# Output weights split in place during the sparse attention, their second half read twice, and half of the first output tile's products issued from the first latent pass

## The chip, the core and the metric

The kernel runs on one core of a Trainium2 chip. A core has a matrix engine (TensorE, PE in the rows; PEld is its weight load), a vector engine (VectorE, DVE), a scalar engine (ScalarE, ACT), a general engine (GpSimd, POOL) and a queue for transfers (SyncE, SP), all with instruction streams of their own that meet only in semaphores. The metric is the device time of one launch in microseconds (us), as the median of several runs.

## What is computed

A decoder layer for 512 tokens of width 1024. One projection feeds two causal attentions of 8 heads each: A, where an indexer's scores pick 128 keys for each query, and B, the latent one, with queries and keys of 96 (64 + 32 rotary) channels. Both are gated, set side by side, multiplied by one output matrix and normalised:

```python
h = x @ w_in[l]
...
o_a = _dsa_branch(qa, ka, va, iq, ik, iw) * jax.nn.silu(ga)
o_b = _mla_branch(c_q, c_kv, k_rope, ...) * jax.nn.silu(gb)
out = jnp.concatenate([o_a, o_b], axis=-1) @ w_out[l]
x = _layernorm(DEEPNORM_ALPHA * x + out, ln_g[l], ln_b[l])
```

`w_out` is 1024 x 1024. Its rows 0 to 511 (chunks k = 0 to 3 of 128 rows) meet branch A's output, rows 512 to 1023 (k = 4 to 7) branch B's.

## The kernel before

Products of float32 accuracy are made of three products of a faster type: a matrix is split into a high part (a cast) and a low part (the value minus its high part), and high x high, high x low and low x high are added. So each weight chunk needs a cast and a subtraction before it can be used.

**Order of the work.** After the input projection (to about 170 us) the two attentions run as 64 units, one for each block of 128 queries and head: u = 0 to 31 for A (`NU_A` = 32), u = 32 to 63 for B. A pass is 8 units, one block m with all heads, and blocks come as m = 3, 2, 1, 0 (`ORDER`), each with m + 1 blocks of keys: 512, 384, 256, then 128 columns. Each engine has one loop over u, and its instruction order is fixed there. In iteration u, PE makes `scores(u)` (L1196 and L1199 in A, L1205 in B), `transposes(u - 2)` (L1255), `outputs(u - 4)` (L1271 in A, L1286 in B), and then output products if it is their turn. DVE masks the scores (`mask_unit`, L858; the scores come from PSUM, the mask from SBUF), in B also subtracts a low part (`probs_low`, L898), reads and merges head pairs (L913, L288), and once a pass normalises and gates (L874, L875, L884). ACT exponentiates (L583) and copies the transposes out (L603). `scores(u)` waits for `mask_unit(u - 2)`; transposes wait for the exponential.

**The output weights.** `w_out` comes in eight loads of 512 KB, one for each k, with two chunks j = 2k and 2k + 1 (its left and right 512 columns). They land in the ring `w_raw` (RING = 8 chunks of 2 KB a partition). The first four loads are issued at u = 8; the other four each wait until POOL has made the low parts of the ring slots that they overwrite. High parts `wo_hi`: of j = 0 to 7 by DVE in iterations 12 to 19 (`wo_high`, L936, one each), of j = 8 to 15 by ACT in iterations 38 to 45 (`split_hi`, L470). Low parts (`wo_lo_a`, `wo_lo_b`): all 16 by POOL (L431), which waits first until all 32 scores of A are made, since `wo_lo_a` and `wo_lo_b` lie where A's transposed keys lie.

**Output products.** For output tile i (one block of queries) PE makes 48 products (L1329), 8 chunks k x 2 halves x 3. Of tile 0 they stand in iterations 47 to 54 (`OUT_AT[0]` = 47), six in each, of tile 1 from 55, of tile 2 from 63. The operand `oT` is the gated output, transposed by `o_transposes` (L1300), then copied (ACT, L615) and its low part taken (DVE, L890); its first half (branch A) for tile 0 is made in iteration 45.

**POOL** has, in this order: rotary work of the latent queries, the low parts of B's values (`vb_parts`, L415, two operations), the 16 low parts of `w_out` with `scale_gate(0)` among them, then B's later pairs.

## Time and profile before

| | us |
|---|---|
| median of 3 runs | 321.32 (321.14 to 323.02) |
| profiled execution: span from first to last instruction | 318.7 |
| TensorE busy | 298.5 (94%) |
| VectorE busy | 248.5 (78%) |
| ScalarE busy | 177.9 (56%) |
| GpSimd busy | 146.0 (46%) |

The span is that of one profiled execution; the median holds in addition what lies around the first and last instruction. The chain that ended last goes through PE for 70% and through DVE for 18% of the span. Busy shares are means over stages with different limits, so the stretches of the two attentions are read apart.

### The profile page before, as it was taken

Reading aid. Unit: us, or ns where it says so; the run is one execution under the profiler, and the core shown is the slowest. Engines: PE = TensorE matmul, PEld = TensorE weight load, DVE = VectorE, ACT = ScalarE, POOL = GpSimd, SP = SyncE. Lnnn points to the kernel's source line nnn. Section 1 sums busy time; section 2 is a strip of 40 time slices with the busy share of each in tenths; the row PEclk is TensorE's granted clock in tenths of the full one; section 3 lists DMA queues with packets and bytes.
Section 4 is the critical chain, followed back from the end, with each engine's and each line's share of the span. In section 5 each row is a group of like instructions: output and inputs, shape, how many; then the busy total and the mean of one; then the engine's idle time right before and its main releaser. Section 6 shows DMA issues by size and latency. Waiting matters only on the chain.

```text
span 318.7 us, 5232 instructions
## 1 busy us (share of the span) xinstructions
PE 298.5 (94%) x1646; PEld 253.2 (79%) x1646; DVE 248.5 (78%) x613; ACT 177.9 (56%) x419; POOL 146.0 (46%) x163
## 2 busy tenths in 40 slices
PE   8869979999999999999999999999987899999991
PEld 7859968688888888887888789997654688888891
DVE  2968997888999999997053645865999967888685
ACT  5834244478234244366267787998878855554200
POOL 4858635310999994434326600020797310334311
PEclk9999999999999999999999999999999999999998
DMA  7947440300144433320055004230150340030311
GB/s 255 325 119 205 127 134 12 112 11 0 56 143 134 130 77 126 98 67 2 0 132 134 1 0 148 120 60 0 54 200 13 89 176 0 3 133 2 132 66 66
DMA packets 14202, 29.16 MB, mean 91 GB/s; under 512 B 1664, under 2 KB 4224, under 8 KB 14176
## 3 DMA queue, kind: packets, MB, share of 16 engines
q1 hardware_dynamic: 13904, 28.53, 29.0%
q10 hardware_dynamic: 272, 0.30, 0.3%
q8 instruction: 13, 0.21, 0.3%
q14 instruction: 13, 0.11, 0.1%
HBM read 24.18 MB, written 2.10 MB: 82 GB/s over the span
## 4 chain that ended last, share of the span: by engine, by line
PE 70%; DVE 18%; issue 4%; ACT 4%; DMA 2%; POOL 1%; DVEq 0%; SPq 0%; ACTq 0%; POOLq 0%
PE ps L1047 34%; PE ps L1329 14%; PE ps L1271 5%; PE ps L1255 5%; PE ps L1205 3%; PE ps L1196 2%; DVE tmp L731 2%; DMA w_raw<-in_w_in 2%; PE ps L1286 2%; PE ps L1199 2%; DVE tmp L732 1%; DVE idx_tok L734 1%; DVE trig_tmp L715 1%; DVE lat_tok L781 1%; DVE probsT_b L898 1%
## 5 line engine op out<-in xcount | busy, mean ns | idle before, releaser
L389 POOL TENSOR_TENSOR w_lo<-w_raw,w_hi 128x512 fp32r<-128x512 f32 (+3 forms) x62 | 76.1, 1245 | 47.3 <-ACT w_hi L470 47.3
L1047 PE MATMUL ps<-w_hi,x_hi 128*128 128x512 f32 (+2 forms) x220 | 83.2, 378 | 4.6 <-issue 3.7
L1047 PE MATMUL ps<-w_hi,x_lo 128*128 128x512 f32 (+2 forms) x220 | 82.0, 373 | 0.0
L1047 PE MATMUL ps<-w_lo,x_hi 128*128 128x512 f32 (+2 forms) x220 | 81.9, 372 | 0.0
L470 ACT ACTIVATE w_hi<-w_raw 128x512 fp32r<-128x512 f32 (+3 forms) x62 | 36.2, 592 | 68.9 <-PE ps L1047 68.0
L1047 PEld LDWEIGHTS ps<-w_hi,x_hi 128*128 128x128 f32 x220 | 41.4, 188 | 11.6 <-issue 5.0
L1047 PEld LDWEIGHTS ps<-w_hi,x_lo 128*128 128x128 f32 x220 | 41.3, 188 | 6.5
L1047 PEld LDWEIGHTS ps<-w_lo,x_hi 128*128 128x128 f32 x220 | 41.4, 188 | 5.9
L1329 PE MATMUL ps<-wo_hi,oT 128*128 128x512 f32 (+1 forms) x144 | 44.5, 371 | 0.0
L583 ACT ACTIVATE probs<-probs,small 128x512 f32<-128x512 f32 (+3 forms) x64 | 35.7, 559 | 11.7 <-DVE small L858 11.3
L1255 PE MATMUL ps<-ident,probs 128*128 128x128 f32 x160 | 28.5, 276 | 3.5 <-ACT probs L583 2.1
L1255 PEld LDWEIGHTS ps<-ident,probs 128*128 128x128 f32 x160 | 19.5, 140 | 14.6 <-DVE probsT_b L898 8.8
L1329 PEld LDWEIGHTS ps<-wo_hi,oT 128*128 128x128 f32 x144 | 26.1, 189 | 4.0
L812 DVE MATCH_REPLACE8 score<-small,score 128x256 f32<-128x256 f32 (+2 forms) x48 | 25.7, 550 | 0.0
L809 DVE MAX8 small<-score 128x8 f32<-128x256 f32 (+2 forms) x48 | 23.7, 555 | 0.0
L1205 PE MATMUL ps<-kbT,qbT 96*128 96x512 f32 (+3 forms) x64 | 23.2, 443 | 0.5 <-DVE small L858 0.5
L858 DVE CUSTOM_DVE_ANT_0 probs<-ps,causal 128x128 f32<-128x128 f32 (+3 forms) x40 | 17.7, 444 | 6.8 <-PE ps L1205 4.1
L858 DVE CUSTOM_DVE_ANT_0 probs<-ps,score 128x512 f32<-128x512 f32 (+2 forms) x24 | 13.3, 556 | 12.4 <-PE ps L1199 12.3
L415 POOL TENSOR_TENSOR vb_parts<-vb,vb_parts 128x512 fp32r<-128x512 f32 x2 | 2.9, 1470 | 42.3 <-ACT vb_parts L625 42.3
L1271 PE MATMUL ps<-va,probsT 128*128 128x64 f32 x160 | 21.4, 264 | 0.0
L1271 PEld LDWEIGHTS ps<-va,probsT 128*128 128x128 f32 x160 | 20.5, 193 | 0.6 <-issue 0.6
L288 POOL TENSOR_TENSOR obT<-half_sum,crossed 64x128 f32<-64x128 f32 x16 | 8.6, 538 | 26.8 <-DVE oT L890 15.6
(168 smaller groups left out, 583.3 us busy)
## 6 DMA issues: line engine op xcount, KB each, us to landing
w_raw<-in_w_in SPq DMA_DIRECT2D x20, 512.0 KB, 3.6
w_raw<-in_w_out SPq DMA_DIRECT2D x8, 512.0 KB, 4.3
kaT_swap<-kaT SPq DMA_DIRECT2D x8, 256.0 KB, 3.7
x_res<-in_x SPq DMA_DIRECT2D x4, 512.0 KB, 5.4
w_raw<-in_w_in SPq DMA_DIRECT2D x4, 416.0 KB, 4.1
x_raw<-in_xT SPq DMA_DIRECT2D x3, 512.0 KB, 5.5
out_y<-y SPq DMA_DIRECT2D x6, 256.0 KB, 2.0
w_raw<-in_w_in SPq DMA_DIRECT2D x3, 296.0 KB, 5.8
```

The costliest lines, as they stand in the source:

```text
L288: eng.tensor_tensor(obT[rows, g % 4], half_sum[rows, g % 2, a], crossed[rows, g % 2], ALU.add).then_inc(pair_merged, 1)
L389: pool.tensor_tensor(w_lo[:, s, 0:n], w_raw[:, s, 0:n], w_hi[:, s, 0:n], ALU.subtract).then_inc(w_lo_ready, 1)
L470: act.activation(dst, w_raw[:, s, 0:n], ACT.Copy).then_inc(w_hi_ready, 1)
L583: act.activation(probs[:, u % NPROBS, 0:N], probs[:, u % NPROBS, 0:N], ACT.Exp, bias=neg_max[:, u % 8:u % 8 + 1], scale=-1.0, accum_out=ro ...
L809: step(V.max(top8[:, 8 * j:8 * j + 8], sc))
L812: step(V.match_replace(out=sc, in_to_replace=top8[:, 8 * j:8 * j + 8], in_values=sc, imm_value=TAKEN))
L858: V.tensor_tensor_reduce(out=probs[:, u % NPROBS, 0:N], in0=ps_s[:, u % 2, 0:N], in1=bias, scale=-scale, scalar=3.0e38, op0=ALU.add, op1=A ...
L1047: ins = mm(dst, a, b, start=start and j == 0, stop=stop and j == len(pairs) - 1)
L1205: ins = mm(ps_s[:, b, 0:N], qbT[:, h, t], kbT[:, h, 0:N], start=True, stop=True)
L1255: ins = nc.tensor.transpose(bank[:, j * P:(j + 1) * P], probs[:, u % NPROBS, j * P:(j + 1) * P], ident[:, :])
L1271: ins = mm(ps_o[:, v % 2, h * A_DIM:(h + 1) * A_DIM], probsT[:, u % 3, j * P:(j + 1) * P], va[:, j, h * A_DIM:(h + 1) * A_DIM], start=(j = ...
L1329: ins = mm(out_ps(i, b), oT[i % 2][:, o, k, :], w[:, wcols], start=(r == 0), stop=(r == 3 * KT - 1))
```

## The change

- SP: after the first four loads of `w_out` come, at once, k = 4 and 5 into a new buffer `wo_early` (two chunk pairs), then the copy of the rotary keys (L334, L343 after), then k = 6 and 7 into the same buffer, each once DVE has cast the pair that lay there (`wo_hi_ready` of 10 and 12). When A's scores are made (u = 31 done), k = 4 to 7 are read a second time, into `wo_raw_b`, where A's keys lay, without further waits. 2 MB are read more.
- DVE casts all 16 chunks, in iterations 12 to 27 (before: 8 in 12 to 19). ACT casts none.
- POOL subtracts j = 0 to 7 in place in `w_raw` as soon as each is cast, ahead of the two `vb_parts` operations; j = 8 to 15 in place in `wo_raw_b`, behind them, then `scale_gate(0)`.
- The A half of tile 0: `o_transposes`, the ACT copy and the DVE low part stand in iteration 31 (`O_FIRST` + `T_LAG`; before 45), and its 24 products (k = 0 to 3, both halves) in iterations 34 to 41, three in each. Iterations 47 to 54 keep the other 24, three in each.
- `x_res`, `lng` and `lnb` move to other addresses; their loads follow the second reading.

```diff
-    O_AFTER = [NU_A + HEADS * (i + 1) + OT_AT - T_LAG for i in range(TT - 1)] + [NU]
+    O_AFTER = [[NU_A + HEADS * (i + 1) + OT_AT - T_LAG + b for b in range(2)] for i in range(TT - 1)] + [[NU, NU]]
+    O_AFTER[0][0] = O_FIRST
...
-    wo_lo_a = sb("wo_lo_a", 178, [P, KT // 2, 2, BANK], f32r)
+    wo_lo_a = sb("wo_lo_a", 64, [P, RING, BANK], f32r)
+    wo_early = sb("wo_early", 80, [P, 2, 2, BANK])
+    wo_raw_b = sb("wo_raw_b", 98, [P, KT // 2, 2, BANK])
...
+        def out_steps(i):
+
+            split = ((0, KT // 2), (KT // 2, KT)) if i == 0 else ((0, KT),)
+            return [(b, k, j) for k0, k1 in split for b in range(len(PIECES[i])) for k in range(k0, k1) for j in range(3)]
...
+            sp.wait_ge(acc_ready, A_END)
+            for k in range(KT // 2, KT):
+                if k >= KT // 2 + 2:
+                    sp.wait_ge(wo_hi_ready, 2 * k - 2)
+                sp.dma_start(wo_early[:, k % 2], w_out_v[:, k]).then_inc(early_loaded[k % 2], 16)
+                if k == KT // 2 + 1:
+                    sp.wait_ge(acc_read[2], ACC_LAST[2])
+                    sp.dma_start(kbT[NOPE:B_QK, 1:B_HEADS, :],
...
-            for q in range(C_OUT // 2 + RPAIR, len(LOADS)):
-                load(q)
-            sp.wait_ge(w_lo_ready, C_OUT + 2 * KT)
+            sp.wait_ge(scores_ready, NU_A)
+            for k in range(KT // 2, KT):
+                sp.dma_start(wo_raw_b[:, k - KT // 2], w_out_v[:, k]).then_inc(raw_b_loaded[k - KT // 2], 16)
...
+            for j in range(KT):
                 c = C_OUT + j
                 pool.wait_ge(w_loaded[(c // 2) % RPAIR], 16 * (c // 2 // RPAIR + 1))
-                wait_wo_hi(pool, j)
-                if j == 0:
-                    pool.wait_ge(scores_ready, NU_A)
+                pool.wait_ge(wo_hi_ready, j + 1)
                 pool.tensor_tensor(wo_lo(j // 2, j % 2), w_raw[:, c % RING, :], wo_hi[:, j // 2, j % 2],
                                    ALU.subtract).then_inc(w_lo_ready, 1)
-                if j == SCALE_AT:
-                    scale_gate(0)
...
+            for j in range(KT, 2 * KT):
+                k = j // 2
+                pool.wait_ge(raw_b_loaded[k - KT // 2], 16)
+                pool.wait_ge(wo_hi_ready, j + 1)
+                pool.tensor_tensor(wo_lo(k, j % 2), wo_raw_b[:, k - KT // 2, j % 2], wo_hi[:, k, j % 2],
+                                   ALU.subtract).then_inc(w_lo_ready, 1)
+            scale_gate(0)
...
-                if 0 <= u - WO_LATE < RING:
-                    split_hi(C_OUT + RING + u - WO_LATE)
...
-                V.tensor_copy(wo_hi[:, j // 2, j % 2], w_raw[:, c % RING, :]).then_inc(wo_hi_ready, 1)
+                if k < KT // 2:
+                    dve.wait_ge(w_loaded[(c // 2) % RPAIR], 16 * (c // 2 // RPAIR + 1))
+                    src = w_raw[:, c % RING, :]
+                else:
+                    dve.wait_ge(early_loaded[k % 2], 16 * ((k - KT // 2) // 2 + 1))
+                    src = wo_early[:, k % 2, j % 2]
+                V.tensor_copy(wo_hi[:, k, j % 2], src).then_inc(wo_hi_ready, 1)
...
-                if 0 <= u - WO_EARLY < RING:
+                if 0 <= u - WO_EARLY < 2 * KT:
                     wo_high(u - WO_EARLY)
...
+                if 0 <= u - A_HALF_AT < HEADS:
+                    out_products(0, 3 * (u - A_HALF_AT), 3 * (u - A_HALF_AT + 1))
                 for t in range(TT - 1):
                     if 0 <= u - OUT_AT[t] < HEADS:
-                        out_products(t, per * (u - OUT_AT[t]), per * (u - OUT_AT[t] + 1))
+                        rest, first = (per, 0) if t > 0 else (per // 2, 3 * KT)
+                        out_products(t, first + rest * (u - OUT_AT[t]), first + rest * (u - OUT_AT[t] + 1))
...
+O_FIRST = 29
+A_HALF_AT = 34
```

VectorE in iterations 20 to 22 of the sparse attention, before (the two ISA rows are one mask with its read-out):

```order
L858 ISA probs,small<-ps,score 128x256
L858 ISA small 128x1
L874 RECIPROCAL small<-small 128x8
L875 TENSOR_TENSOR o_norm<-ps,small 128x512
L858 ISA probs,small<-ps,score 128x256
L858 ISA small 128x1
L884 TENSOR_TENSOR gate<-o_norm,gate 128x512
L858 ISA probs,small<-ps,score 128x256
L858 ISA small 128x1
```

and the same place of the changed kernel:

```order
L868 ISA probs,small<-ps,score 128x256
L868 ISA small 128x1
L884 RECIPROCAL small<-small 128x8
L885 TENSOR_TENSOR o_norm<-ps,small 128x512
L951 CAST wo_hi<-wo_early 128x512
L868 ISA probs,small<-ps,score 128x256
L868 ISA small 128x1
L894 TENSOR_TENSOR gate<-o_norm,gate 128x512
L951 CAST wo_hi<-wo_early 128x512
L868 ISA probs,small<-ps,score 128x256
L868 ISA small 128x1
L951 CAST wo_hi<-wo_early 128x512
```

Each of the iterations 20 to 27 has gained a cast behind its mask. GpSimd from the last rotary operation to the first pair, before:

```order
L415 TENSOR_TENSOR vb_parts_94<-vb,vb_parts_94 128x4x128
L415 TENSOR_TENSOR vb_parts_93<-vb,vb_parts_93 128x4x128
L431 TENSOR_TENSOR wo_lo_a<-w_raw,wo_hi 128x512 x8
L431 TENSOR_TENSOR wo_lo_b<-w_raw,wo_hi 128x512 x5
L423 TENSOR_TENSOR gate<-gate,small 128x512
L431 TENSOR_TENSOR wo_lo_b<-w_raw,wo_hi 128x512 x3
```

and now:

```order
L434 TENSOR_TENSOR wo_lo_a<-w_raw,wo_hi 128x512 x8
L438 TENSOR_TENSOR vb_parts_96<-vb,vb_parts_96 128x4x128
L438 TENSOR_TENSOR vb_parts_95<-vb,vb_parts_95 128x4x128
L444 TENSOR_TENSOR wo_lo_b<-wo_raw_b,wo_hi 128x512 x8
L428 TENSOR_TENSOR gate<-gate,small 128x512 x2
```

Eight subtractions have moved ahead of the value parts, from the latent attention into the sparse one. PE in iteration 35, now with three output products behind the outputs (before, the score row followed directly):

```order
L1222 MATMUL ps<-kbT,qbT 128x512
L1272 MATMUL ps<-ident,probs 128x128 x4
L1288 MATMUL ps<-va,probsT 128x64
L1345 MATMUL ps<-wo_hi,oT_66 128x512
L1345 MATMUL ps<-wo_lo_a,oT_66 128x512
L1345 MATMUL ps<-wo_hi,oT_66 128x512
```

The same three rows stand in each of the iterations 34 to 41, and 24 rows are gone from iterations 47 to 54.

## Rows read from the trace of the kernel before

**Rows 1.** Head of the page.

```profile
span 318.7 us, 5232 instructions
```

**Rows 2.** Busy time by stretch; (x) counts instructions, then PE's granted clock and transfers.

```profile
core 0: us, PE busy (x) PEld busy (x) DVE busy (x) ACT busy (x) POOL busy (x), PEclk, DMA share, GB/s
202.00:219.60 17.60, 17.42 (x152) 16.90 (x151) 13.03 (x54) 15.94 (x56) 1.67 (x1) 1.00 0.14 27
...
222.00:237.40 15.40, 14.14 (x80) 9.32 (x78) 14.29 (x31) 12.58 (x32) 12.52 (x10) 1.00 0.30 103
237.40:249.35 11.95, 9.37 (x50) 6.07 (x51) 11.42 (x28) 11.08 (x30) 9.09 (x8) 1.00 0.13 46
...
253.10:270.70 17.60, 17.60 (x100) 15.09 (x99) 12.75 (x38) 9.89 (x30) 1.05 (x1) 1.00 0.31 108
```

**Rows 3.** VectorE in order of time, iterations 12 to 28: start, duration, line, operation, count, [idle before].

```profile
202.04 0.43 DVE L936 CAST wo_hi<-w_raw 128x512 fp32r<-128x512 f32 x1
...
202.98 0.69 DVE L884 TENSOR_TENSOR gate<-o_norm,gate 128x512 f32<-128x512 f32 x1
...
210.44 0.42 DVE L858 CUSTOM_DVE_ANT_0 probs<-ps,score 128x256 f32<-128x256 f32 x1 [0.36 <-PE ps L1199]
...
212.57 0.42 DVE L858 CUSTOM_DVE_ANT_0 probs<-ps,score 128x256 f32<-128x256 f32 x1
...
214.02 0.29 DVE L858 CUSTOM_DVE_ANT_0 probs<-ps,causal 128x128 f32<-128x128 f32 x1 [0.44 <-PE ps L1199]
...
217.25 0.29 DVE L858 CUSTOM_DVE_ANT_0 probs<-ps,causal 128x128 f32<-128x128 f32 x1 [0.46 <-PE ps L1199]
```

**Rows 4.** VectorE and GpSimd side by side, in order of time.

```profile
33.77 1.41 POOL L389 TENSOR_TENSOR w_lo<-w_raw,w_hi 128x512 fp32r<-128x512 f32 x1 [0.92 <-ACT w_hi L470]
34.05 1.27 DVE L755 CAST iq_st<-idx_tok 128x256 fp32r<-128x256 f32 x1
...
226.12 10.46 POOL L431 TENSOR_TENSOR wo_lo_a<-w_raw,wo_hi 128x512 fp32r<-128x512 f32 x8
230.03 0.68 DVE L898 TENSOR_TENSOR probsT_b<-ps,probsT_b 128x512 fp32r<-128x512 f32 x1
230.63 1.03 DVE L884 TENSOR_TENSOR gate<-o_norm,gate 128x512 f32<-128x512 f32 x1
```

**Rows 5.** Operations on `wo_hi`: ns min/median/max, first and last start.

```profile
L936 DVE CAST wo_hi<-w_raw x8: 419/421/427, 202.0 to 209.7; 128x512 fp32r<-128x512 f32 x8
L431 POOL TENSOR_TENSOR wo_lo_a<-w_raw,wo_hi x8: 1267/1279/1732, 226.1 to 235.3; 128x512 fp32r<-128x512 f32 x8
L470 ACT ACTIVATE wo_hi<-w_raw x8: 612/614/616, 233.0 to 249.3; 128x512 fp32r<-128x512 f32 x8
```

**Rows 6.** Pair merges, VectorE: ns min/median/max of one; two of them from the timeline.

```profile
L288 DVE TENSOR_TENSOR obT<-half_sum,crossed x16: 282/290/1264, 234.8 to 268.3; 64x128 f32<-64x128 f32 x16
...
239.77 1.03 DVE L288 TENSOR_TENSOR obT<-half_sum,crossed 64x128 f32<-64x128 f32 x2
...
243.74 1.55 DVE L288 TENSOR_TENSOR obT<-half_sum,crossed 64x128 f32<-64x128 f32 x2
```

**Rows 7.** Two pieces of the chain that ended last: start, length, what.

```profile
246.62 0.50 ACT wo_hi L470
...
251.85 1.38 PE ps L1329 x6
```

**Rows 8.** PE: scores of iterations 42, 47 and 48, from the timeline.

```profile
237.38 0.91 PE L1205 MATMUL ps<-kbT,qbT 96*128 96x384 f32 x2 [0.50 <-DVE small L858]
...
249.35 0.81 PE L1205 MATMUL ps<-kbT,qbT 96*128 96x384 f32 x2
...
253.07 0.59 PE L1205 MATMUL ps<-kbT,qbT 96*128 96x256 f32 x2
```

**Rows 9.** Transfers: KB each, median us from issue to landing.

```profile
w_raw<-in_w_in SPq DMA_DIRECT2D x20, 512.0 KB, 3.6
...
lnb<-in_ln_b SPq DMA_DIRECT2D x1, 512.0 KB, 6.4
```

More of the change, by code:

```diff
@@ L165, in wo_lo @@
     def wo_lo(k, half):
-        return (wo_lo_a if k < KT // 2 else wo_lo_b)[:, k % (KT // 2), half]
+        return wo_lo_a[:, (C_OUT + 2 * k + half) % RING] if k < KT // 2 else wo_lo_b[:, k - KT // 2, half]
     def y_of(i):
@@ L197, in build @@
         pos_loaded, norm_g_loaded, ln_loaded = sem("pos_loaded"), sem("norm_g_loaded"), sem("ln_loaded")
+        early_loaded = [sem(f"early_loaded{i}") for i in range(2)]
+        raw_b_loaded = [sem(f"raw_b_loaded{i}") for i in range(KT // 2)]
         xres_loaded = [sem(f"xres_loaded{i}") for i in range(2)]
@@ L423, in scale_gate @@
                 pool.tensor_tensor(g3, g3, rinv.unsqueeze(2).broadcast_to([P, HEADS, V_DIM]), ALU.mult).then_inc(gate_scaled, 1)
[L425 removed]
+            for j in range(KT):
                 c = C_OUT + j
                 pool.wait_ge(w_loaded[(c // 2) % RPAIR], 16 * (c // 2 // RPAIR + 1))
[L428 to L430 removed]
+                pool.wait_ge(wo_hi_ready, j + 1)
                 pool.tensor_tensor(wo_lo(j // 2, j % 2), w_raw[:, c % RING, :], wo_hi[:, j // 2, j % 2],
                                    ALU.subtract).then_inc(w_lo_ready, 1)
[L433 to L434 removed]
+            for j in (3, 2):
+                pool.wait_ge(vb_hi_ready, VB_ORDER.index(j) + 1)
+                pool.tensor_tensor(vb_parts[j][:, :, 1:3], vb[:, j, :].rearrange("p (q a d) -> p q a d", a=2, d=V_DIM),
+                                   vb_parts[j][:, :, 0:4:3], ALU.subtract).then_inc(vb_lo_pool, 1)
+            for j in range(KT, 2 * KT):
[5 more added lines that the diff above has]
+            scale_gate(0)
             def root(i):
@@ L462, in split_hi @@
                 act.wait_ge(w_loaded[(c // 2) % RPAIR], 16 * (c // 2 // RPAIR + 1))
-                if c >= C_OUT:
-                    k, half = divmod(c - C_OUT, 2)
-                    dst = wo_hi[:, k, half]
-                else:
-                    dst = w_hi[:, s, 0:n]
-                    if c >= RING:
-                        wait_chunk_used(act, c - RING)
+                dst = w_hi[:, s, 0:n]
+                if c >= RING:
+                    wait_chunk_used(act, c - RING)
                 act.activation(dst, w_raw[:, s, 0:n], ACT.Copy).then_inc(w_hi_ready, 1)
@@ L606, in copy_oT_hi @@
                 n = slot_of[i, b]
+                if i == 0 and b == 0:
+                    act.wait_ge(wo_hi_ready, 2 * KT)
                 if i >= 2 and b == 0:
@@ L639, in _ @@
                 i, j = divmod(u - NU_A, HEADS)
-                if 0 < i < TT and j == OT_AT:
+                if u == O_FIRST + T_LAG:
+                    copy_oT_hi(0, 0)
+                if 1 < i < TT and j == OT_AT:
                     copy_oT_hi(i - 1, 0)
@@ L997, in _ @@
                     evac_qpeT(u - PET_AT - 1)
-                if 0 <= u - WO_EARLY < RING:
+                if 0 <= u - WO_EARLY < 2 * KT:
                     wo_high(u - WO_EARLY)
-                if 0 < i and j == OT_AT:
+                if u == O_FIRST + T_LAG:
+                    copy_oT_lo(0, 0)
+                if 1 < i and j == OT_AT:
                     copy_oT_lo(i - 1, 0)
@@ L1303, in out_products @@
             def out_products(i, a, z):
-                last = i == TT - 1
+                last, steps = i == TT - 1, out_steps(i)
                 for n in range(a, z):
-                    b, r = divmod(n, 3 * KT)
-                    k, j = divmod(r, 3)
+                    b, k, j = steps[n]
+                    r = 3 * k + j
                     cols = PIECES[i][b]
@@ L1314, in out_products @@
                         pe.wait_ge(oT_lo_ready, 2 * i + 1 + (k > 0))
-                    if n == 0:
-                        if i == 0:
-                            pe.wait_ge(w_lo_ready, C_OUT + 2 * KT)
+                    if i == 0 and n in (0, 3 * KT):
+                        pe.wait_ge(w_lo_ready, C_OUT + (KT if n == 0 else 2 * KT))
                     if r == 0:
```

32 lines of the change are left out of this document (10 added, 22 removed).

## The prediction

> **What bounds the kernel now.** I read the page first (span 318.7 us [rows 1]), then busy time by stretch, then the timelines of the two attentions, and last the chain of waits at the seams.
>
> In the sparse attention, iterations 12 to 31, TensorE is busy 17.42 of 17.60 us [rows 2] and sets the pace. VectorE has small gaps there: in iterations 20, 24 and 28 it waited 0.36, 0.44 and 0.46 us for scores ahead of its mask [rows 3]. That is the cover for anything added to VectorE. GpSimd is nearly empty, 1.67 us.
>
> The latent attention has three parts. Iterations 34 to 41 are the stretch from 222.0 to 237.4, where the scores of 42 begin [rows 8]: TensorE is busy 14.14 of 15.40 us, idle 1.26 [rows 2]. Iterations 42 to 46 take 11.95 us for five, 2.39 each, with TensorE busy only 9.37 and VectorE 11.42, ScalarE 11.08 [rows 2]: this is the hole. The chain there runs through ScalarE's cast of `wo_hi`, 0.50 us a time [rows 7], and through VectorE's work. Iteration 47 takes 3.72 us (249.35 to 253.07 [rows 8]). Iterations 48 to 54, seven of 17.60 us in sum, 2.51 each, are TensorE's again: 17.60 busy of 17.60 [rows 2], 1.38 us of each being six output products [rows 7].
>
> **What the change takes from the sparse attention.** Three terms.
>
> (a) GpSimd now subtracts while VectorE casts. The two don't overlap: a cast of 128x256 that began at 34.05 under a GpSimd subtraction (33.77 to 35.18) took 1.27 us and ended 0.14 after it; the gate of 230.63 took 1.03 instead of 0.69 beside GpSimd, while the low part at 230.03, which reads PSUM, took its usual 0.68 [rows 3, 4]. One of the merges of 290 ns took 1264 [rows 6]. The mask reads PSUM too, so it is not held up; the casts and the gate are. The Trainium skill, SBUF — State Buffer, section Who interferes with whom, says that a cast in a two-port mode or a VectorE operation with two SBUF inputs shares a port pair with GpSimd, and the first to start has it for its whole instruction. By that rule all the 128x512 casts are held up, which is a wider claim than the one 128x256 cast that the trace shows; were they not, the sum would be that of the first rival below.
>
> Each subtraction waits for its cast and then runs 1.279 us [rows 5]; the next cast comes behind one mask, 0.5 us later, and finds GpSimd at work. So cast and subtraction alternate: 1.28 plus 0.27 (twice the 0.14, for twice the width) to 0.42 (a whole cast [rows 5]), 1.55 to 1.70; I take 1.62. The first subtraction starts at 202.5 (cast 0 at 202.04 [rows 3]) and ends at 203.8; the gate, due at 202.98, ends at 204.4 behind it, cast 1 at 204.7, and cast 7 six rounds later at 204.7 + 6 x 1.62 = 214.4. The mask of iteration 20 follows cast 7. It stood at 210.44 [rows 3]: +4.0 us. With 1.55 and 1.70 it is +3.5 and +4.5; TensorE can't hide it, since scores of u wait for the mask of u - 2, and it has no other work.
>
> (b) In iterations 20 and 21, cast 8 waits for subtraction 7 (ends about 215.7), so it ends at 216.0. The value part, now behind the eight, takes GpSimd then for 1.3 us and the gate of iteration 21 waits for it (217.4, ending at 218.0), then cast 9, 218.3. The mask of 22 follows: 218.3 - 214.4 = 3.9 us after that of 20, where it was 212.57 - 210.44 = 2.1 [rows 3]. +1.8 us; bounds 0.5 (two casts bare, 0.84, less one gap) and 2.6.
>
> (c) k = 6 may be loaded only after cast 9, and cast 12 needs it. A 512 KB load takes 3.6 us to land, up to 6.4 [rows 9]. Issued at 218.4 it lands at 222.0. Iteration 24's mask would stand at about 219.7 (1.45 us after that of 22, as 214.02 - 212.57 [rows 3]) and its cast at 220.0: it waits 2.0 us, and behind it on VectorE wait the masks of 25 and 26, for which TensorE's scores wait. k = 7, issued after cast 11 (219.7), lands at 223.3, about when cast 14 comes. From there four casts and masks at VectorE's pace bring mask 28 to about 224.4, 4.7 us after mask 24, where it was 217.25 - 214.02 = 3.2 [rows 3]: +1.5; bounds 0.8 and 4.3 (6.4 us to land).
>
> (d) The moved transposes, copy and low part of iteration 31 cost up to 0.7 on VectorE; TensorE's lead over the masks at the end gives about as much back. In sum 4.0 + 1.8 + 1.5 = 7.3, less 0.3 for TensorE's lead: **+7.0**, bounds 4.5 and 11.
>
> The other additions are free. The loads of k = 4 and 5 are needed ten iterations later. The second reading goes out when A's scores are made, at 219.6 in the old count [rows 2], where GpSimd is through with the value parts at 226.1 [rows 4]; 6.5 us are more than one load takes. The eight late subtractions lie under iterations 34 to 41, where VectorE will have slack. Without that cover they would cost what they do now, some 1.4 us.
>
> **What it gives back in the latent attention.** The 24 moved products are 0.23 us each (1.38 for six [rows 7]), 0.69 an iteration.
>
> - Iterations 34 to 41: +5.5 us of products, into 1.3 us of idle time [rows 2]; modelled ends hide some more idle time. **+3.7**, bounds 3.2 and 4.3. This half of the work moves from a full TensorE to a full TensorE.
> - Iterations 42 to 46: ScalarE loses five casts of 0.61 [rows 5] and is no bound. VectorE's 11.42 us hold about 1.4 us of waiting on GpSimd (two pairs of merges, 1.03 and 1.55 us instead of 0.6 [rows 6]) and 0.7 for the low part moved away: 9.35, 1.87 an iteration, against TensorE's 1.4 (2.51 less 1.38 is 1.13 for 256 keys; for 384 I estimate 0.3 more). So VectorE sets 9.35 against 11.95: **-2.6**, bounds -1.6 and -3.6.
> - Iteration 47: 3.72 becomes about 2.0 (TensorE's 1.3, between 1.13 and 1.4, and 0.69). **-1.7**.
> - Iterations 48 to 54: 2.51 - 0.69 = 1.82. VectorE has 12.75 us in seven, 1.82 as well [rows 2], so not all of 7 x 0.69 = 4.8 comes: **-4.2**, bounds -2.5 and -4.8.
>
> Sum: +3.7 - 2.6 - 1.7 - 4.2 = **-4.8**, bounds -1.5 and -6.9. Tiles 1 to 3 and the tail are unchanged.
>
> **The sum.** 318.7 + 7.0 - 4.8 = 320.9 us of span. The median of the runs shown, 321.32, is 2.6 us over the span of the profiled execution, so 323.5.
>
> **The rivals.**
>
> 1. *The casts slip by GpSimd.* Then (a) and (b) fall to the gaps: eight more casts of 0.34 to 0.42 in iterations with 0.4 us of slack, about +0.5; cast 12 comes at 214.4, its load, issued at 211.4, lands at 215.0, +1.0 for both late loads; 0.3 for iteration 31. +1.8 - 4.8 = -3.0 with the low bound of the gain, -5.1 with the high one: 316 to 318. For it: none of the 128x512 casts has been seen under GpSimd. Against: [rows 4]. Chance 0.20, with the case that the gain is at its upper bound.
> 2. *VectorE stays the bound of the latent attention*, the other side. The place is iterations 42 to 54: where VectorE needs 2.0 us in 42 to 46 and 2.2 in 48 to 54, since it also waits for ScalarE's copies in each round, the gain there is 2.0 + 1.5 + 2.1 = 5.6 against +3.7, -1.9 in sum: 318.7 + 7.0 - 1.9 + 2.6 = 326.4. It decides from 0.15 us an iteration more than I take. For it: VectorE busy 11.42 of 11.95. Chance 0.20.
> 3. *The loads of k = 6 and 7 are late.* At 6.4 us each, (c) is 4.3 instead of 1.5: 326.3. Against: nothing else moves then. Chance 0.10.
> 4. *The change does not do what it says*: the products move between two full stretches and the hole stays, because it was VectorE's and not ScalarE's. Then 42 to 46 stay at 11.9: 326.1. Chance 0.05.
>
> **How the numbers follow.** My forecast, 322 to 324.5 and down to 318 where (b) and (c) are at their low bounds, has 0.45. About 1% (3.2 us) is what a measurement of this kernel can tell from no change. Faster by over 1% (under 318.1) is rival 1, 0.20. Slower (over 324.5) are rivals 2, 3 and 4, 0.35. The range goes from 317.5 (most of rival 1 left in) to 328 (two of the slower bounds together left out).
>
> **What would show it.** (a) right: the casts of iterations 13 to 19 last 1.0 to 1.3 us in the rows instead of 0.42, GpSimd's subtractions alternate with them, and the mask of iteration 20 starts near 214.4. (b): the gate of iteration 21 at over 1 us. (c): VectorE idle 1 to 2 us on a transfer ahead of cast 12. The latent attention: iterations 34 to 41 near 19 us, 42 to 46 near 9.4, 48 to 54 near 13.4, no ScalarE cast in the chain. TensorE's idle time should have moved from 237-249 to 204-224. I am wrong if the casts stay at 0.42 under GpSimd, or if the first score of B starts before 224 or after 230 (it was 219.6).

## The result, and the profile after

The changed kernel takes **329.46 us** (median, 328.48 to 334.31) against 321.63 (321.14 to 323.02) before: a ratio of 1.0222, interval 1.0175 to 1.0269. It is slower, by 7.8 us, clear of noise; the forecast was 323.5 with a range up to 328. One of its four executions, 334.31, ran in a slower state at a lower mean clock (0.961, against 0.974 to 0.981 in the others), and the median of the other three is 329.19. The profiled execution has a span 8.7 us longer than that of [rows 1]. In every execution the time is 1.8 or 1.9 us over the span, so differences of medians and of spans can be compared.

The page's head, and its rows of TensorE's busy share and granted clock in 40 equal slices of 8.2 us (9 is 90% or more):

```profile
span 327.4 us, 5237 instructions
PE   7869989999999999999999999878999979899990
...
PEclk9979999999999999999999999998799999999998
```

TensorE's idle time does move, out of the latent attention into the slices at 205 to 229 us, as forecast. What the forecast had nothing of is the second row: behind those slices the granted clock drops.

Busy time by stretch, columns as in [rows 2]; the first row answers to the first of [rows 2]:

```profile
202.00:219.60 17.60, 15.07 (x111) 12.85 (x109) 17.47 (x34) 11.64 (x34) 11.46 (x9) 1.00 0.31 96
...
219.70:226.37 6.67, 4.72 (x36) 4.22 (x37) 3.71 (x19) 3.87 (x16) 0.00 (x0) 0.97 0.48 157
226.37:233.78 7.41, 7.41 (x29) 5.65 (x30) 3.89 (x16) 4.83 (x19) 0.00 (x0) 0.57 0.47 168
233.78:252.69 18.91, 18.91 (x103) 14.05 (x103) 15.25 (x35) 13.03 (x32) 11.67 (x9) 1.00 0.44 157
252.69:260.26 7.57, 7.55 (x47) 5.76 (x46) 7.21 (x23) 6.72 (x20) 1.05 (x1) 1.00 0.02 3
260.26:264.90 4.64, 2.49 (x14) 1.57 (x13) 4.34 (x11) 3.38 (x9) 0.00 (x0) 1.00 0.00 0
264.90:277.61 12.71, 12.71 (x78) 11.05 (x77) 9.93 (x30) 8.66 (x26) 1.05 (x1) 1.00 0.00 0
```

VectorE is now the full engine of the sparse attention (17.47 of 17.60 us, before 13.03) and TensorE has gaps (15.07, before 17.42). The second row is masks 22 to 28, the third mask 28 to score 34, and the last four are iterations 34 to 41, 42 to 46, 47, and 48 to 54. By iteration, with the forecast beside it (up to iteration 28 between starts of masks on VectorE, from 34 on between starts of scores on TensorE; all in us):

| stage | before | after | difference | forecast |
|---|---|---|---|---|
| up to mask 2 | 183.35 | 184.42 | +1.07 | 0 |
| masks 2 to 13 | 19.15 | 19.15 | 0 | 0 |
| masks 13 to 20 (a) | 7.94 | 12.40 | +4.46 | +4.0 |
| masks 20 to 22 (b) | 2.13 | 3.73 | +1.60 | +1.8 |
| masks 22 to 28 (c) | 4.68 | 6.67 | +1.99 | +1.5 |
| mask 28 to score 34 (d) | 4.77 | 7.41 | +2.64 | -0.3 |
| scores 34 to 42 | 15.36 | 18.91 | +3.55 | +3.7 |
| scores 42 to 47 | 11.97 | 7.57 | -4.40 | -2.6 |
| scores 47 to 48 | 3.72 | 4.64 | +0.92 | -1.7 |
| scores 48 to 55 | 17.49 | 12.71 | -4.78 | -4.2 |
| scores 55 to 56 | 2.29 | 3.41 | +1.12 | 0 |
| the rest | 45.85 | 46.38 | +0.53 | 0 |

The differences make 8.7 us, the forecast column 2.2. So 6.5 us are to be explained, and most of them lie in five rows: (d) 2.9, iteration 47 2.6, iteration 55 1.1, the start 1.1, and in the other direction iterations 42 to 46 with 1.8.

**The sparse attention.** VectorE in order of time, columns as in [rows 3]:

```profile
204.05 1.46 DVE L894 TENSOR_TENSOR gate<-o_norm,gate 128x512 f32<-128x512 f32 x1
...
206.24 1.30 DVE L951 CAST wo_hi<-w_raw 128x512 fp32r<-128x512 f32 x1
207.47 0.54 DVE L868 CUSTOM_DVE_ANT_0 probs<-ps,score 128x384 f32<-128x384 f32 x1
...
207.94 1.31 DVE L951 CAST wo_hi<-w_raw 128x512 fp32r<-128x512 f32 x1
...
223.11 0.43 DVE L951 CAST wo_hi<-wo_early 128x512 fp32r<-128x512 f32 x1 [1.76 <-DMA wo_early<-in_w_out]
...
225.49 0.43 DVE L951 CAST wo_hi<-wo_early 128x512 fp32r<-128x512 f32 x1 [1.19 <-DMA wo_early<-in_w_out]
```

and GpSimd beside it:

```profile
205.99 1.27 POOL L434 TENSOR_TENSOR wo_lo_a<-w_raw,wo_hi 128x512 fp32r<-128x512 f32 x1 [1.03 <-DVE wo_hi L951]
207.69 1.27 POOL L434 TENSOR_TENSOR wo_lo_a<-w_raw,wo_hi 128x512 fp32r<-128x512 f32 x1 [0.43 <-DVE wo_hi L951]
209.39 1.27 POOL L434 TENSOR_TENSOR wo_lo_a<-w_raw,wo_hi 128x512 fp32r<-128x512 f32 x1 [0.43 <-DVE wo_hi L951]
```

Six of the eight casts of j = 0 to 7, 0.42 us each before [rows 5], take 1.30 to 1.44 under GpSimd; the other two (0.43 and 0.41) met no subtraction. The gate of 0.69 takes 1.46, while the mask between them, which reads PSUM, keeps its 0.54. Cast and subtraction alternate in a cycle of exactly 1.70 us (207.69, 209.39): 1.27 of subtraction and 0.43 until the next one. The cast of 206.24 ends at 207.54, 0.28 behind the end of the subtraction that it met, and the next subtraction begins 0.15 later. The two transfers of 1.76 and 1.19 us are the late k = 6 and 7.

**The clock.** PE's granted clock around the seam, busy time by stretch again:

```profile
220.00:224.00 4.00, 3.06 (x25) 2.81 (x25) 2.23 (x12) 2.61 (x10) 0.00 (x0) 1.00 0.71 223
224.00:226.00 2.00, 1.47 (x12) 1.22 (x11) 0.81 (x5) 1.04 (x6) 0.00 (x0) 0.98 0.20 78
226.00:232.00 6.00, 5.83 (x22) 4.60 (x23) 3.48 (x15) 3.84 (x15) 0.00 (x0) 0.50 0.32 108
232.00:234.00 2.00, 2.00 (x10) 1.47 (x9) 1.00 (x3) 1.42 (x4) 0.00 (x0) 0.81 0.87 332
```

For 6.8 us (225.9 to 232.8) TensorE ran at the lower of its two levels, 1.2 instead of 2.4 GHz, in iterations in which it sets the pace again. It had been idle for 4.3 of the 23 us before, in gaps of 0.2 to 0.5 us and around the two late loads. In the kernel before, the clock is 1.00 throughout these stretches.

**Iteration 47.** TensorE in order of time:

```profile
261.65 0.60 PE L1303 MATMUL ps<-probsT_b,vb_parts 128*128 128x256 f32 x3
264.13 0.47 PE L1345 MATMUL ps<-wo_hi,oT 128*128 128x512 f32 x1 [1.88 <-issue]
```

and the chain of waits there (start, length, what):

```profile
261.93 0.03 ACT probsT_b L611
261.95 0.36 issue
262.31 0.63 ACT oT L625
262.94 1.18 issue
264.13 0.93 PE ps L1345 x3
```

The first product of iteration 47 is now k = 4, the first that needs the B half of `oT`. That half is copied in the same iteration (262.31 on ScalarE) and its low part taken behind it (263.35 to 264.03 on VectorE). Before the change the twelve products of k = 0 to 3 came first, in iterations 47 and 48: there, in the trace of before, the low part of the B half was ready at 253.63 and its first product (k = 4) began at 256.70:

```profile
252.95 0.68 DVE L890 TENSOR_TENSOR oT<-obT,oT 128x512 fp32r<-128x512 f32 x1
...
256.70 0.40 PE L1329 MATMUL ps<-wo_hi,oT 128*128 128x512 f32 x1
256.93 0.40 PE L1329 MATMUL ps<-wo_lo_b,oT 128*128 128x512 f32 x1
```

Now the six products have become three, and the gap in front of them is 1.88 us.

### The profile page after: what moved, and what is told of

The parts are those of the page before. It is cut to its first block, busy times and chain, and to the rows that moved or that the text cites. A ratio compares the mean times of both kernels' runs of the same rounds, so it can differ in the third digit from the quotient of the medians.

```text
span 327.4 us, 5237 instructions
## 1 busy us (share of the span) xinstructions
PE 304.0 (93%) x1646; PEld 257.8 (79%) x1646; DVE 254.6 (78%) x621; ACT 175.4 (54%) x411; POOL 145.4 (44%) x163
## 4 chain that ended last, share of the span: by engine, by line
PE 69%; DVE 18%; issue 5%; DMA 3%; SPq 1%; ACT 1%; POOL 1%; DVEq 0%; ACTq 0%; POOLq 0%
PE ps L1064 36%; PE ps L1345 13%; PE ps L1222 5%; PE ps L1272 4%; PE ps L1288 3%; PE ps L1303 3%; DVE wo_hi L951 2%; DMA w_raw<-in_w_in 2%; DVE probs L868 2%; DVE tmp L741 2%; DVE tmp L742 1%; DMA wo_early<-in_w_out 1%; PE ps L1213 1%; DVE lat_tok L791 1%; DVE iq_st L765 1%
## 5 line engine op out<-in xcount | busy, mean ns | idle before, releaser
L1064 PE MATMUL ps<-w_hi,x_lo 128*128 128x512 f32 (+2 forms) x220 | 82.9, 377 | 0.0
L1064 PEld LDWEIGHTS ps<-w_hi,x_hi 128*128 128x128 f32 x220 | 42.1, 191 | 11.8 <-issue 6.0
L1345 PE MATMUL ps<-wo_hi,oT 128*128 128x512 f32 (+1 forms) x144 | 46.1, 373 | 1.9 <-issue 1.9
L1064 PEld LDWEIGHTS ps<-w_hi,x_lo 128*128 128x128 f32 x220 | 42.0, 191 | 6.5
L819 DVE MAX8 small<-score 128x8 f32<-128x256 f32 (+2 forms) x48 | 23.5, 545 | 0.0
L1288 PEld LDWEIGHTS ps<-va,probsT 128*128 128x128 f32 x160 | 21.5, 200 | 0.9 <-issue 0.9
L1288 PE MATMUL ps<-va,probsT 128*128 128x64 f32 x160 | 22.2, 271 | 0.0
L434 POOL TENSOR_TENSOR wo_lo_a<-w_raw,wo_hi 128x512 fp32r<-128x512 f32 x8 | 10.2, 1274 | 25.3 <-DVE wo_hi L951 25.3
L611 ACT ACTIVATE probsT_b<-ps 128x512 fp32r<-128x512 f32 (+3 forms) x32 | 13.8, 431 | 12.5 <-PE ps L1272 12.2
```

What stands on the lines that cost most here:

```text
L611: act.activation(dst, ps_pT[:, slot_of[u] % 2, 0:N], ACT.Copy).then_inc(probsT_copied, 1)
L819: step(V.max(top8[:, 8 * j:8 * j + 8], sc))
L1064: ins = mm(dst, a, b, start=start and j == 0, stop=stop and j == len(pairs) - 1)
L1288: ins = mm(ps_o[:, v % 2, h * A_DIM:(h + 1) * A_DIM], probsT[:, u % 3, j * P:(j + 1) * P], va[:, j, h * A_DIM:(h + 1) * A_DIM], start=(j = ...
L1345: ins = mm(out_ps(i, b), oT[i % 2][:, o, k, :], w[:, wcols], start=(r == 0), stop=(r == 3 * KT - 1))
```

## The experiments

My theory after the two traces: four losses, each with a place of its own. Casts and subtractions exclude each other (a), the loads of k = 6 and 7 are late (c), TensorE's gaps then bring its clock down (d), and iteration 47 waits for copies that its old products used to hide. Against it stand single causes: the clock falls because of the late loads or of the transfers at the seam; and the latent attention gains nothing from the products, only from ScalarE's lost casts. The stages below are those of the table. Each stage time comes from the one profiled execution of its kernel; the name in brackets is the one by which the expectations call a kernel.

**All sixteen subtractions late.** (`e1_late_sub`)

```diff
+            vb_low_pool(3)
+            pool.wait_ge(scores_ready, NU_A)
             for j in range(KT):
...
-            for j in (3, 2):
...
+                if j == 3:
+                    vb_low_pool(2)
...
-A_HALF_AT = 34
+A_HALF_AT = 40
```

> The changed kernel with GpSimd's eight early subtractions held back until all scores of the sparse attention are made (the value parts before and between them), and the first half's products in iterations 40 to 47 instead of 34 to 41, so that they have their low parts. Port theory (casts and gate on VectorE and subtractions on GpSimd exclude each other; cost 4.5 us in iterations 12 to 20 and 1.6 in 20 to 22): the casts fall to 0.42 us, the mask of iteration 20 comes about 7.9 us after that of 13 instead of 12.4, and the median falls by 6 us to about 323.5; to 321 if TensorE's clock then stays up as well. The late loads still cost about 2 us. GpSimd is then busy beside the merges of the latent attention, up to 1.5 us back. Rival (the second reading or the moved products make the loss): within 1 us of 329.5.

324.25 us (323.65 to 325.12), ratio 1.0081 (1.0055 to 1.0107). Casts in the sparse attention, ns min/median/max:

```profile
L955 DVE CAST wo_hi<-w_raw x8: 420/422/427, 204.3 to 211.9; 128x512 fp32r<-128x512 f32 x8
L955 DVE CAST wo_hi<-wo_early x8: 414/420/426, 213.9 to 222.7; 128x512 fp32r<-128x512 f32 x8
```

Masks 13 to 20 take 7.94 us, as before the change: (a) is the exclusion and nothing else, since the casts in these iterations are the same as before. The clock stays at 1.00 from 204 to 232 and mask 28 to score 34 takes 5.10. The two late loads remain (1.73 and 1.09 us), so a load wait alone did not bring the clock down here. This is the profiled execution, with a mean clock of 0.986; four of the other five had 0.970 to 0.980, so the clock was lower for longer in those, and where in them is not known. (b) remains too, 3.77 us, without any subtraction:

```profile
214.39 1.28 POOL L432 TENSOR_TENSOR vb_parts<-vb,vb_parts 128x512 fp32r<-128x512 f32 x1 [31.19 <-DVE wo_hi L955]
...
214.56 1.64 DVE L898 TENSOR_TENSOR gate<-o_norm,gate 128x512 f32<-128x512 f32 x1
```

GpSimd's first value part began 0.17 us ahead of the gate, which took 1.64 instead of 0.69. In return iterations 42 to 46 take 11.86 us instead of 7.57: their products stand there now, and GpSimd subtracts beside the merges.

**Value parts two iterations later** (`e7_late_sub_vb22`), on top of it.

```diff
-VB_EARLY = 20
+VB_EARLY = 22
```

> As e1_late_sub (all sixteen subtractions late), but GpSimd's two value parts are let go two iterations later (VB_EARLY 22 for 20). In e1_late_sub the mask of iteration 22 stood 3.77 us behind that of 20 (2.13 before); there GpSimd's first value part (1.28 us) had begun 0.17 us ahead of the gate, which took 1.64. My theory: that collision is most of the 1.6 us: iterations 20 to 22 fall to 2.1 to 2.6, and the median from 324.25 to about 322.8. Rival (the casts of iterations 20 and 21 themselves, which stand behind gate and read-out, make the time): 20 to 22 stays at 3.5 or more and the median at 324.2.

324.01 us (322.82 to 324.80), ratio 1.0073 (1.0052 to 1.0095). The gate took 0.69 and masks 20 to 22 fell from 3.77 to 2.81 (I had 2.1 to 2.6), so 0.96 of (b)'s 1.6 us is that one collision; the 0.7 that is left goes with the two casts behind read-out and gate. The median moved by 0.2 only: in the profiled execution the granted clock now dipped (0.73 in 220 to 224, 0.68 in 224 to 226 us) and mask 28 to score 34 took 6.18 instead of 5.10. My place was right, my forecast of the time missed.

**Four subtractions early, twelve late** (`e8_four_early`), against the kernel with all of them late.

```diff
-            vb_low_pool(3)
-            pool.wait_ge(scores_ready, NU_A)
             for j in range(KT):
...
                 if j == 3:
+                    vb_low_pool(3)
+                    pool.wait_ge(scores_ready, NU_A)
                     vb_low_pool(2)
```

> As e1_late_sub, but the first four subtractions stand beside the casts as in the changed kernel, the other twelve late. It tells the price of one round and where the granted clock begins to fall. My theory (price in proportion): iterations 13 to 20 take 7.94 plus the gate's 0.9 plus three to four rounds of 0.4 to 0.5, about 10.2 (12.40 with eight, 7.94 with none); the granted clock stays at 1.00 since TensorE's idle time is half that of the changed kernel; median about 326. Rival (any idle time there brings the clock down): the granted clock shows 0.5 somewhere between 218 and 235 us and the median is 327.5 or more.

325.94 us (323.98 to 327.40), ratio 1.0121 (1.0079 to 1.0164). Masks 13 to 20: 9.85, between 7.94 and 12.40. The gate took 1.45, three casts 1.30, 1.31 and 1.44, the next 0.42: the price is by the collision. The median is what I expected, but the clock was my miss: in the profiled execution it stood at 0.50 from 225.3 to 235.6 us. The four executions ran from 323.98 at a mean clock of 0.991 to 327.40 at 0.972, so the fall seems to come in some executions of this kernel and not in others.

**Loads of k = 4 and 5 first** (`e2_reload_early`), casts in the order 8 to 11, 0 to 7, 12 to 15, so that k = 6 and 7 are loaded long before their casts.

```diff
+CAST_ORDER = [8, 9, 10, 11, 0, 1, 2, 3, 4, 5, 6, 7, 12, 13, 14, 15]
...
-                    wo_high(u - WO_EARLY)
+                    wo_high(CAST_ORDER[u - WO_EARLY])
```

> The changed kernel with the casts in the order j = 8 to 11, 0 to 7, 12 to 15 and the loads of k = 4 and 5 issued first, so that those of k = 6 and 7 go out eight iterations sooner. Late-load theory: VectorE's two waits for wo_early (1.76 and 1.19 us) vanish, -2.0. Clock theory (the granted clock fell to 0.50 from 225.9 to 232.5 us because TensorE had stood still between 216 and 226): the clock stays at 1.00 there and another 2.3 us go, 325.2. Rival (that fall of the clock is chance, or comes from the exclusion alone): 327.5. The port cost of 6 us stays in either case.

326.98 us (326.28 to 328.01), ratio 1.0166 (1.0128 to 1.0204). The waits for transfers are gone, and masks 13 to 28 take 20.45 instead of 22.80. The clock fell all the same, earlier:

```profile
216.00:220.00 4.00, 2.48 (x17) 1.98 (x16) 4.00 (x8) 1.74 (x6) 2.55 (x3) 0.97 0.00 0
220.00:224.00 4.00, 4.00 (x21) 4.00 (x21) 4.00 (x13) 2.20 (x9) 3.05 (x3) 0.50 0.00 0
```

Ahead of the fall the longest wait of TensorE was 0.78 us. So the fall needs neither the late loads nor one long gap. The Trainium skill, TensorE: Matmul & The Clock Gate, section A second HAM failure mode: psum-queue depth-cycling, tells of a kernel whose many short idle times between groups of matmuls make the clock go between its two levels; this trace agrees, with one fall and one return (219.8 to 230.0 us).

**TensorE's gaps filled.** (`e9_filled`) The changed kernel, but with the outputs of A issued again in iterations 14 to 27; each repeat starts its sum anew.

```diff
-                    for j in range(m + 1):
+                    for _ in range(1 + REPEAT.get(u + PV_LAG, 0)):
+                        for j in range(m + 1):
...
+REPEAT = {**{u: 1 for u in range(14, 20)}, **{u: 2 for u in range(20, 24)}, **{u: 5 for u in range(24, 28)}}
```

> The changed kernel, but TensorE issues the outputs of A once more in iterations 14 to 19, twice more in 20 to 23 and five times more in 24 to 27 (each repeat starts its sum anew, so that the values stay the same). Everything else, the collisions of casts and subtractions and the late loads included, is left. It asks for the cause of the granted clock's fall to 0.50 behind the slow stretch. My theory (the fall follows from TensorE's idle time between 203 and 226 us, 4.3 us of 23 in the changed kernel): with most of that time filled the granted clock stays at 0.95 or above from 204 to 236 us, the masks 28 to 31 and the scores 32 to 34 come back to about 2.1 and 2.4 us, iterations 13 to 28 take up to 1 us more for the added work, and the median is 328 to 329. Rival (the clock falls for another reason, such as the transfers or the A-to-B seam): 0.50 shows for about 6 us again, and the median is 330 or more.

337.14 us (336.71 to 337.68), ratio 1.0486 (1.0462 to 1.0510). Masks 13 to 22 take 12.40 and 3.73 us, as in the changed kernel, so there the repeats are free; from 22 on I had counted half the matmuls that one output issues, and masks 22 to 28 take 14.96, 8.3 us more. This is why the time missed. The question it was made for has an answer:

```profile
212.00:216.00 4.00, 4.00 (x38) 4.00 (x37) 4.00 (x9) 2.35 (x7) 3.15 (x3) 1.00 0.55 101
216.00:220.00 4.00, 4.00 (x38) 4.00 (x38) 3.97 (x9) 2.60 (x9) 3.24 (x3) 1.00 0.00 0
...
236.00:240.00 4.00, 3.82 (x25) 2.77 (x24) 2.69 (x10) 3.06 (x13) 0.00 (x0) 1.00 0.39 110
```

With the same collisions and the same transfers, but a busy TensorE, the clock is 1.00 in every stretch from 204 to 240, and mask 28 to score 34 takes 5.11 instead of 7.41 us. The fall in the sparse attention follows from the idle time, and it costs 2.3 us. The other 0.3 over before's 4.77 stays; about half of it goes with iteration 31's transposes and copies (5.11 us with them and 4.96 without in the last kernels below), the rest is open. The other three executions had mean clocks of 0.981 to 0.986, none below the profiled one's 0.981. This kernel has its fall later: 0.50 from 271.9 to 275.3 us, behind iteration 47's gap of 1.88 us.

**The rest of tile 0's products from iteration 49** (`e3_rest_at_49`), four in each of six.

```diff
-                for t in range(TT - 1):
+                if 2 <= u - OUT_AT[0] < HEADS:
+                    out_products(0, 3 * KT + 4 * (u - OUT_AT[0] - 2), 3 * KT + 4 * (u - OUT_AT[0] - 1))
+                for t in range(1, TT - 1):
```

> The changed kernel with the second half's 24 products of tile 0 in iterations 49 to 54, four in each, instead of 47 to 54, three in each. Theory: in iteration 47 the first of them (k = 4) waits for the copies of the B half of oT, which are made in that same iteration; 1.9 us of TensorE's idle time. Then iteration 47 takes 2 us or less instead of 4.6, the six products that it and 48 held cost 1.4 later, net -1.2: 328.3. Rival (iteration 47 waits for VectorE's masks whatever stands in it): 329.5, with the same 4 us there.

326.93 us (325.82 to 327.91), ratio 1.0161 (1.0120 to 1.0202), 2.5 less than the changed kernel. Iteration 47 takes 1.83, 48 to 54 14.21, 55 2.99: together 1.7 less, where I had 1.2. The wait was a loss, not work moved.

**Tile 0's products back** (`e4_products_back`) where they were, weights as changed.

```diff
-    O_AFTER[0][0] = O_FIRST
...
-                if u == O_FIRST + T_LAG:
-                    o_transposes(0, 0)
...
-                if 0 <= u - A_HALF_AT < HEADS:
-                    out_products(0, 3 * (u - A_HALF_AT), 3 * (u - A_HALF_AT + 1))
...
-                        rest, first = (per, 0) if t > 0 else (per // 2, 3 * KT)
-                        out_products(t, first + rest * (u - OUT_AT[t]), first + rest * (u - OUT_AT[t] + 1))
+                        out_products(t, per * (u - OUT_AT[t]), per * (u - OUT_AT[t] + 1))
```

> The changed kernel with the whole first output tile's products back in iterations 47 to 54, six in each, and its transposes and copies back in iteration 45; weights, casts, loads and subtractions as changed. Theory by stage: -3.5 us in iterations 34 to 41, the hole of 42 to 46 about 1 us longer than in the changed kernel, 48 to 54 +4.8: 330.5, so the move of the products is worth about 1 us. Rival (the moved products are what costs): 325 or less.

329.59 us (329.50 to 331.33), ratio 1.0257 (1.0217 to 1.0298). Scores 34 to 56 take 48.46 us, against 47.24 changed and 50.83 before. So by stages the products' move in the changed kernel seems worth 1.2 us and the lost ScalarE casts with the earlier subtractions 2.4; by medians the move is worth 0.1. The split is rough: in this profiled execution (331.33 us, 1.7 over the median) the clock was at 0.50 from 221.9 to 238.9 us, 4.2 us into iterations 34 to 41, and in the changed kernel's not at all there.

**Everything laid around the collisions.** (`e5_gap_casts`) Casts of j = 8 to 15 in iterations 5 to 12, where a unit has 512 or 384 keys and TensorE more to do, 0 to 7 in 13 to 20; loads in the same order; GpSimd's early subtractions behind the gate of iteration 21; the rest of the products from 49.

```diff
+            pool.wait_ge(o_ready, 2)
             for j in range(KT):
...
-                if 0 <= u - WO_EARLY < 2 * KT:
-                    wo_high(u - WO_EARLY)
+                if u in CAST_AT:
+                    wo_high(CAST_AT[u])
...
-WO_EARLY = 12
+CAST_AT = {**{5 + n: 8 + n for n in range(8)}, **{13 + n: n for n in range(8)}}
+CAST_ORDER = [CAST_AT[u] for u in sorted(CAST_AT)]
```

> The changed kernel, with the work on the output weights laid elsewhere: the casts of chunks 8 to 15 stand in iterations 5 to 12 and those of 0 to 7 in 13 to 20, one each; the transfers of k = 4 to 7 go out ahead of those of k = 0 to 3; GpSimd's eight early subtractions wait until the gate of iteration 21 is through, so that they meet no cast and no gate. The rest of tile 0's products stands in iterations 49 to 54, four in each, so that none needs the oT half of its own iteration. My theory (each loss of the changed kernel has its own place: cast against subtraction, a late load, the dip of the granted clock behind TensorE's idle time, the copy that iteration 47 waits for): iterations 13 to 20 about 8, no transfer waited for, granted clock 1.00 from 204 to 235 us, sparse part at most 1 us longer than before, iterations 34 to 56 about 1.3 us shorter than before: median 320 to 322.5. Rival (the second reading of 2 MB, the longer sparse pass with 16 casts and the subtractions in GpSimd's later part cost by themselves): the sparse part 3 us or more longer than before with no cast above 0.5 us, median 324 or more.

**317.31 us** (317.06 to 317.71), ratio 0.9858 (0.9844 to 0.9873): 4.35 us less than before and 12.2 less than the changed kernel, and better than I expected. Its page's head and clock row:

```profile
span 315.3 us, 5237 instructions
...
PEclk9999999999999999999999999999999999999998
```

and its iterations 34 to 41, 42 to 46, and 48 to 54 by busy time:

```profile
223.42:242.34 18.92, 18.92 (x103) 13.99 (x102) 16.41 (x35) 13.95 (x34) 13.69 (x11) 1.00 0.50 188
242.34:249.91 7.57, 7.56 (x47) 5.76 (x46) 7.21 (x23) 6.72 (x20) 1.05 (x1) 1.00 0.01 3
251.73:265.95 14.22, 13.54 (x82) 11.53 (x81) 12.58 (x38) 10.57 (x32) 1.05 (x1) 1.00 0.00 0
```

Masks 13 to 20 take 7.93, 20 to 22 2.47, 22 to 28 4.65, mask 28 to score 34 5.11. From mask 2 to score 34 it takes 1.1 us more than before, for sixteen casts instead of eight and iteration 31's copies. Scores 34 to 56 take 45.51 against 50.83: **-5.3 us**, about what the forecast gave for the latent attention. The same second reading of 2 MB is in it. The spans of the two profiled executions, neither with a dip of the clock at the start, differ by 3.4 us (315.3 against 318.7). The medians' 4.35 holds up to 1 us more, since three of this kernel's four executions have a mean clock of 0.995 and only three of the thirteen of before have that.

**The same with the products back** (`e6_gap_casts_no_products`): the edit of the kernel with the products back, on this one; the first and last lines of it again.

```diff
-    O_AFTER[0][0] = O_FIRST
...
+                        out_products(t, per * (u - OUT_AT[t]), per * (u - OUT_AT[t] + 1))
```

> As e5_gap_casts, but the whole of tile 0's products and its transposes and copies are back where they were before the change (transposes in iteration 45, six products in each of 47 to 54). It measures the move of the products where nothing else disturbs it. My theory: the move gains about 1.2 us by stages (48.46 against 47.24 us in iterations 34 to 56), so this kernel takes about 1 us more than e5_gap_casts: 321.5 to 323.5, with iterations 34 to 41 at about 15.4 and 48 to 54 at 17.5. Rival (the casts that ScalarE lost are what helps the second latent pass, the products' move gives nothing): the same time as e5_gap_casts within 0.3 us, iterations 42 to 46 below 9.5.

321.43 us (320.18 to 323.08), ratio 1.0000 (0.9981 to 1.0018). Against 317.31 that is 4.1 us in the medians and 3.6 by stages (49.09 and 45.51 in scores 34 to 56), not the 1.0 I expected. But two things went back here, the products of the A half and the start of the rest at 49, and the 1.0 was for the first alone. The next kernel parts them: the move with the rest at 47 is worth 1.7 in the medians (321.43 against 319.73), the start at 49 the other 2.4. The weights' handling by itself gives nothing in the sum: scores 34 to 56 take 1.7 less than before, mask 2 to score 34 takes 1.0 more. Iterations 42 to 46 take 9.77 here, against 11.97 before and 7.57 with the products moved.

**The same with the rest at 47.** (`e10_gap_casts_rest_at_47`)

```diff
-                if 2 <= u - OUT_AT[0] < HEADS:
-                    out_products(0, 3 * KT + 4 * (u - OUT_AT[0] - 2), 3 * KT + 4 * (u - OUT_AT[0] - 1))
-                for t in range(1, TT - 1):
+                for t in range(TT - 1):
```

> As e5_gap_casts, but the rest of tile 0's products stands in iterations 47 to 54, three in each, as in the changed kernel. One edit, measured in the kernel in which the sparse pass and the clock are undisturbed. My theory (iteration 47's first product waits for the copy of the oT half made in the same iteration, and that gap isn't given back): iteration 47 takes 4.6 us again, 48 to 54 12.7, 55 3.4, together 1.7 us more than e5_gap_casts, median 319.0. Rival (the wait is only moved, since TensorE has the same work): within 0.4 us of e5_gap_casts, 317.3 to 317.7.

319.73 us (319.26 to 321.00), ratio 0.9954 (0.9937 to 0.9971): 2.4 more than 317.31. Iteration 47 takes 4.64 again. In the profiled execution the clock falls here too, behind the one gap:

```profile
252.00:256.00 4.00, 2.12 (x13) 1.71 (x12) 3.03 (x9) 2.33 (x6) 0.00 (x0) 0.94 0.00 0
256.00:260.00 4.00, 4.00 (x18) 3.38 (x17) 1.82 (x6) 1.47 (x4) 0.00 (x0) 0.63 0.00 0
```

Iterations 48 to 54 take 14.30 in this execution instead of the 12.71 of the changed kernel, where the clock stayed at 1.00 behind the same gap of 1.88 us. But this execution is the slowest of ten (321.00); seven have a mean clock of 0.990 or 0.991, six of them at 319.26 to 319.74. The profiled one, with a dip at the start (20.0 to 23.5 us) and this fall, has 0.986, and the kernel with the rest at 49, with neither, 0.995. So the 0.7 beyond my 1.7 fits one short stretch of low clock in most executions. Whether that is the dip at the start or this fall no trace shows.

## Why the prediction was wrong, step by step

- **(a), right.** +4.46 for +4.0, inside 3.5 to 4.5. The alternation is as described; the cycle is the upper bound of 1.70, not 1.62. The held cast ends 0.28 behind the subtraction, as the 0.27 had it; the sum lacked the 0.15 from the cast's end to the next subtraction. By the rule of the Trainium skill (SBUF — State Buffer, Who interferes with whom), which was the wider claim, the 128x512 casts are held up wherever GpSimd has the ports first; the trace agrees with it for the six that met a subtraction. Rival 1 is out.
- **(b), right in size, and in part in its mechanism.** +1.60 for +1.8; the value part did meet the gate (1.43 us instead of 0.69). A later start of it removed 0.96 in the kernel with late subtractions, and 0.7 went with two casts that met nothing.
- **(c), right.** +1.99 for +1.5, waits of 1.76 and 1.19 us where I had 2.0 and none.
- **(d), the step that failed first.** "TensorE's lead over the masks at the end gives about as much back": it gave nothing back, because the idle time that (a) to (c) put into TensorE took its clock to 1.2 GHz just where it becomes the bound again. +2.64 for -0.3; 2.3 of it is the clock (7.41 us, and 5.11 with the gaps filled). I had costed the slow stretch as a delay only, and read PEclk in the rows of before as a constant.
- **Rival 3** (both loads landing late by 6.4 us each) is out with (c)'s size.
- **Iterations 34 to 41, right** (+3.55 for +3.7). **42 to 46, too cautious** (-4.40 for -2.6): I let VectorE set 1.87 us an iteration, but 7.57 for five is 1.51, TensorE busy 7.55. VectorE's busy time fell by 4.2 (11.42 to 7.21), and I had taken out 2.1. What the low part of iteration 45 takes with it was the term sized too small: 0.7 in my sum, while in the kernels laid around the collisions these iterations take 9.77 us with the transposes and copies of iteration 45 in place and 7.57 with them moved. Rival 2 is out by the same row, and rival 4 too: the hole closed.
- **Iteration 47, the second failed step.** "3.72 becomes about 2.0": it became 4.64. I took away three products of work and didn't ask what the remaining first one waits for: it now waits 1.88 us for the copies of the B half, which twelve other products had covered. With the rest from 49, and so no product in it, the iteration takes 1.83; even with its products' 0.69 and no wait it would be about 2.5, an estimate from these two, and not 2.0. The miss is 2.6 us here, of which 48 to 54 give back 0.6.
- **Iteration 55**, not in the forecast, +1.12. TensorE waits 0.91 us there for `probsT_b` (279.12). Tile 0's read-out and its statistics stand on VectorE just ahead of the mask (276.98 to 278.31), now that the iterations before are shorter; that they are the cause is not shown. It is 2.99 with the rest from 49 and 2.29 with the products back; I haven't tried to undo it.
- **The start**, +1.07: up to 183 us nothing is changed. The granted clock is 0.83 between 20 and 30 us, where the execution of [rows 1] has 1.00. All my profiles but one show such a dip, somewhere from 19 to 27 us, and the mean clocks of other executions of before (0.991 with a span of 319.5 in one) fit it, so it belongs to the executions, not to the change. Why it comes in some is open. Nor is most of it a miss of the forecast of the median: the 2.6 us that I added to the span are 1.8 that lie outside every span and 0.8 by which the execution of [rows 1] is faster than the median. Against the median the forecast missed by 6.0 us, not 6.5.
- **A sign of being wrong** was a first score of B before 224 or after 230: it started at 230.17.

The three forecasts of price in the sparse attention and that of the full TensorE stretch were within 0.5 us each; what was missing were two consequences, 2.9 and 2.6 us. Without them the median would have been about 324. That this is so near 323.5 is partly luck: the 1.8 us that iterations 42 to 46 gave beyond the forecast make up for the smaller misses, iteration 55 and (a) and (c) among them.

## What to carry to other kernels

Where a change makes a full TensorE wait, add to the delay what the granted clock may cost behind it, and read PEclk of the stretches in which TensorE is the bound again. When products are split over two places, look up for each piece which operand it needs first and what work used to lie in front of it. An unused engine is no free one: put GpSimd's SBUF work where VectorE reads PSUM or rests; moving sixteen casts, eight subtractions and the loads, with the rest of the products from iteration 49, turned a loss of 2.2% into a gain of 1.4% (0.5% with the rest at 47).
